# Last product of a decoder trunk: lower rows accumulated as two column halves, last four slices walked row half by row half

## The reference

```python
def rms_norm(x, g):
    return x * rsqrt(mean(x * x, axis=-1) + 1e-6) * g

def conformer_mixer(hn, ...):
    a, g, z = split(hn @ w_in + b_in)            # z has no bias
    u = depthwise_conv(a * sigmoid(g), w_dw) + b_dw      # 31 taps, causal
    u = silu(layer_norm(u, ln_g, ln_b))
    return (u * silu(z)) @ w_out + b_out         # w_out is 2048 x 2048
```

## Time and profile before

| | |
|---|---|
| three runs | 886.42, 886.36, 884.99 us; median 886.36 |
| profiled execution, first to last instruction | 883.1 us |
| what the median has around that | 3.3 us |
| TensorE busy | 860.6 us, 97% of the span |
| VectorE, ScalarE, GpSimd busy | 571.1, 437.5, 346.2 us |
| mean granted TensorE clock | 0.993 of full |
| slices 24 to 31 of the last product | 846.66 to 868.59 us |
| last byte of the last store | about 882.05 us |

### The profile page before, as it was taken

How to read it: one execution, slowest core, us unless ns; L and a number is a source line. 1 busy time by engine, 2 the same in 40 slices (tenths; PEclk the granted TensorE clock), 3 DMA queues, 4 the chain that set the end, 5 groups by cost and what they waited for, 6 DMA issues and landing times.

```text
span 883.1 us, 12265 instructions
## 1 busy us (share of the span) xinstructions
PE 860.6 (97%) x4061; PEld 713.4 (81%) x4061; DVE 571.1 (65%) x922; ACT 437.5 (50%) x603; POOL 346.2 (39%) x173
## 2 busy tenths in 40 slices
PE   9999999999999999999999899999999999899993
PEld 6788888888888888888888688888888888788882
DVE  5655455555555465555554749999999999556554
ACT  6745354454446444454444575444455554474441
POOL 0342004400440014400001588888888788670002
PEclk9999999999999999999999999999999999999997
DMA  9865656555665566646555255555555556447512
GB/s 308 295 191 149 186 161 195 172 168 161 190 176 158 158 182 185 187 142 237 191 191 191 95 187 193 183 179 178 183 185 190 190 162 202 162 164 265 190 48 95
DMA packets 97702, 159.49 MB, mean 181 GB/s; under 512 B 3237, under 2 KB 38917, under 8 KB 97285
## 3 DMA queue, kind: packets, MB, share of 16 engines
q1 hardware_dynamic: 97620, 159.04, 56.0%
q10 hardware_dynamic: 48, 0.02, 0.0%
HBM read 156.94 MB, written 2.10 MB: 180 GB/s over the span
## 4 chain that ended last, share of the span: by engine, by line
PE 94%; DVE 2%; DMA 2%; ACT 0%; POOL 0%; SPq 0%; issue 0%; DVEq 0%
PE acc L358 29%; PE acc L360 29%; PE acc L359 29%; PE X L370 3%; DMA raw<-in_w_in 1%; DVE xrow L996 1%; PE acc L414 1%; DMA xrow<-in_x 1%; PE X L460 1%; DVE c_row L1059 1%; PE X L470 0%; PE X L454 0%; PE X L453 0%; PE X L469 0%; PE X L468 0%; PE X L448 0%
## 5 line engine op out<-in xcount | busy, mean ns | idle before, releaser
L632 ACT ACTIVATE w_hi<-raw 128x1024 fp32r<-128x1024 f32 x288 | 305.2, 1060 | 379.8 <-PE acc L360 376.5
L870 DVE TENSOR_TENSOR w_lo<-raw,w_hi 128x1024 fp32r<-128x1024 f32 x184 | 245.0, 1333 | 235.9 <-ACT w_hi L632 235.6
L358 PE MATMUL acc<-w_hi,xT_hi 128*128 128x512 f32 x876 | 345.8, 395 | 0.8 <-DVE xT_lo L877 0.8
L360 PE MATMUL acc<-w_hi,xT_lo 128*128 128x512 f32 x876 | 341.5, 390 | 0.0
L359 PE MATMUL acc<-w_lo,xT_hi 128*128 128x512 f32 x876 | 341.0, 389 | 0.0
L1152 POOL TENSOR_TENSOR w_lo<-raw,w_hi 128x1024 fp32r<-128x1024 f32 x104 | 252.9, 2436 | 176.3 <-ACT w_hi L632 176.0
L360 PEld LDWEIGHTS acc<-w_hi,xT_lo 128*128 128x128 f32 x876 | 164.4, 188 | 34.9
L358 PEld LDWEIGHTS acc<-w_hi,xT_hi 128*128 128x128 f32 x876 | 164.6, 188 | 33.8 <-DVE xT_lo L877 1.2
L359 PEld LDWEIGHTS acc<-w_lo,xT_hi 128*128 128x128 f32 x876 | 164.7, 188 | 32.6
L1027 DVE SCALAR_TENSOR_TENSOR X<-u_pad,taps,X 128x256 f32<-128x256 f32 x464 | 182.6, 481 | 0.0
L1130 POOL TENSOR_TENSOR rope_t<-q_row,sin_t 128x256 f32<-128x256 f32 x16 | 15.3, 989 | 192.2 <-ACT q_row L640 192.2
(11 more groups left out here) (120 smaller groups left out, 645.1 us busy)
## 6 DMA issues: line engine op xcount, KB each, us to landing
raw<-in_w_in SPq DMA_DIRECT2D x78, 1024.0 KB, 5.3
raw<-in_w_in SPq DMA_DIRECT2D x68, 512.0 KB, 4.4
raw<-in_w_out SPq DMA_DIRECT2D x32, 1024.0 KB, 5.0
gpost<-in_post_g SPq DMA_DIRECT2D x2, 1024.0 KB, 4.6
xrow<-in_x SPq DMA_DIRECT2D x3, 512.0 KB, 9.7
out<-xrow SPq DMA_DIRECT2D x4, 320.0 KB, 3.6
bout<-in_b_out SPq DMA_DIRECT2D x1, 1024.0 KB, 6.8
xrow<-in_x SPq DMA_DIRECT2D x2, 256.0 KB, 4.0
```

What stands on the lines that cost most here:

```text
L358: nc.tensor.matmul(a, hi[:, k, rows], w_hi[:, slot, i], start=(k == 0), stop=False)
L360: last = nc.tensor.matmul(a, lo[:, k, rows], w_hi[:, slot, i], start=False, stop=(k == KT - 1))
L632: nc.scalar.activation(w_hi[:, slot], raw[:, u % LOADS, 2 * half:2 * half + 2], ACT.Copy).then_inc(hi_ready[slot], 1)
L870: nc.vector.tensor_tensor(w_lo[:, slot], raw[:, u % LOADS, 2 * half:2 * half + 2], rd(w_hi, slot), ALU.subtract).then_inc(lo_ready[slot], 1)
```

## The change

The change is in the last product alone, from slice 24 on (column block 3), and in what follows it.

- TensorE: the upper rows still go into `acc[:, 1, 0]` with 512-wide matmuls. The lower rows go into two other PSUM banks, `X[0]` for the left 256 columns of the block and `X[1]` for the right 256, with matmuls 256 wide (`HALVES`, `last_products`). In slices 24 to 27 each slice does upper rows, left half, right half. The last four slices, which fill the ring, are walked three times: upper rows of slices 28 to 31, then the left half of the lower rows of 28 to 31, then the right half. `row0_done` and `half_done` tell of each walk's end.
- The means, the roots and the residual of the two row halves are separate. The lower rows' squares of the last block come in two halves (`ssq_half`), and a small instruction (`part_half`) adds the left one to the mean ahead of the right one.
- VectorE does the whole residual, one row half at a time (`last_residual`): the upper rows in four parts of 512 columns, the lower rows in four of 768, 640, 384 and 256. ScalarE's scaling and GpSimd's addition are gone. SyncE stores each part by itself: eight stores of one row half.

```diff
-OUT_PARTS = [slice(0, 128), slice(128, 384), slice(384, 768), slice(768, 1088), slice(1088, 1408)]
-POOL_COLS = slice(OUT_PARTS[-1].stop, D)
+OUT_PARTS = ([slice(c, c + NCOL) for c in range(0, D, NCOL)],
+             [slice(0, 768), slice(768, 1408), slice(1408, 1792), slice(1792, D)])
+HALVES = (slice(0, NCOL // 2), slice(NCOL // 2, NCOL))
...
-            for n, c in enumerate(OUT_PARTS):
-                sp.wait_ge(o_ready, n + 1)
-                sp.dma_start(ov[:, :, c], xrow[:, :, c]).then_inc(stored, 16)
-                if n in (2, 3):
-                    sp.wait_ge(o_pool, n - 1)
-                    sp.dma_start(ov[:, n - 2, POOL_COLS], xrow[:, n - 2, POOL_COLS]).then_inc(stored, 16)
+            for m in range(MT):
+                for c in OUT_PARTS[m]:
+                    n += 1
+                    sp.wait_ge(o_ready, n)
+                    sp.dma_start(ov[:, m, c], xrow[:, m, c]).then_inc(stored, 16)
...
+            def last_products(s, m, bank, c):
+                slot = s % RING
+                pe.wait_ge(lo_ready[slot], rounds(S_OUT1, 0, 0, s))
+                for i in range(SL_K):
+                    k = SL_K * (s % SLICES) + i
+                    rows = slice(m * P, (m + 1) * P)
+                    nc.tensor.matmul(bank, vT_hi[:, k, rows], w_hi[:, slot, i, c], start=(k == 0), stop=False)
+                    nc.tensor.matmul(bank, vT_hi[:, k, rows], w_lo[:, slot, i, c], start=False, stop=False)
+                    last = nc.tensor.matmul(bank, vT_lo[:, k, rows], w_hi[:, slot, i, c], start=False,
+                                            stop=(k == KT - 1))
+                return last
...
-                slice_products(S_OUT1, 0, 0, s, vT_hi, vT_lo, by_row=(s == 4 * SLICES - 1))
+                if s < 3 * SLICES:
+                    slice_products(S_OUT1, 0, 0, s, vT_hi, vT_lo)
+                elif s < 4 * SLICES - RING:
+                    last_products(s, 0, acc[:, 1, 0], slice(0, NCOL))
+                    for j in range(2):
+                        last = last_products(s, 1, X[j][:, HALVES[j]], HALVES[j])
+                    last.then_inc(w_used[s % RING], 1)
...
+            for s in range(4 * SLICES - RING, 4 * SLICES):
+                last = last_products(s, 0, acc[:, 1, 0], slice(0, NCOL))
+            last.then_inc(row0_done, 1)
+            for j in range(2):
+                for s in range(4 * SLICES - RING, 4 * SLICES):
+                    last = last_products(s, 1, X[j][:, HALVES[j]], HALVES[j])
+                last.then_inc(half_done, 1)
...
-            for m in range(MT):
-                part = yg1[:, m, POOL_COLS]
-                nc.scalar.activation(part, part, ACT.Copy, scale=rms[3][:, m:m + 1]).then_inc(scaled, 1)
+            squares(junk1[:], y1[:, 0, last_col:D], 0, NG - 1, 30)
+            for j in range(2):
+                act.wait_ge(y_ready, MT * (NG - 1) + 2 + j)
+                act.wait_ge(ssq_ready, 31 + j)
+                c = slice(last_col + HALVES[j].start, last_col + HALVES[j].stop)
+                nc.scalar.activation(junk1[:, 0:NCOL // 2], y1[:, 1, c], ACT.Square, accum_out=ssq_half[:, j:j + 1]
+                                     ).then_inc(ssq_ready, 1)
...
-            out1_biased(NG - 1, 1)
-            mean_with_last(32, 2)
-            out1_gained(NG - 1, 1)
+            last_mean(31, 0)
+            last_biased(0)
+            last_gained(0)
             dve.wait_ge(rms_ready, 4)
-            dve.wait_ge(yg_ready, MT * NG)
-            for c in OUT_PARTS:
-                residual(c, 3, yg1, o_ready)
+            dve.wait_ge(yg_ready, MT * (NG - 1) + 1)
+            for c in OUT_PARTS[0][0:3]:
+                last_residual(0, c)
+            dve.wait_ge(ssq_ready, 32)
+            nc.vector.scalar_tensor_tensor(out=part_half, in0=ssq_half[:, 0:1], scalar=1.0 / D,
+                                           in1=mean_part[:, 1:2], op0=ALU.mult, op1=ALU.add).then_inc(half_part, 1)
+            last_biased(1)
+            last_residual(0, OUT_PARTS[0][3])
+            last_gained(1)
+            dve.wait_ge(ssq_ready, 33)
+            dve.wait_ge(half_part, 1)
+            nc.vector.scalar_tensor_tensor(out=mean_sq[:, 1:2], in0=ssq_half[:, 1:2], scalar=1.0 / D,
+                                           in1=part_half, op0=ALU.mult, op1=ALU.add).then_inc(ms_ready, 1)
+            dve.wait_ge(rms_ready, 5)
+            dve.wait_ge(yg_ready, MT * NG + 1)
+            for c in OUT_PARTS[1]:
+                last_residual(1, c)
...
-            inverse_root(rms[3], mean_sq, ms_ready, 4, rms_ready)
             for m in range(MT):
-                pool.wait_ge(scaled, m + 1)
-                c = xrow[:, m, POOL_COLS]
-                nc.gpsimd.tensor_tensor(c, c, yg1[:, m, POOL_COLS], ALU.add).then_inc(o_pool, 1)
+                inverse_root(rms[3][:, m:m + 1], mean_sq[:, m:m + 1], m_half[:, m:m + 1], ms_ready, 4 + m, rms_ready)
```

More of the change, by code:

```diff
@@ L151, in build @@
         mean_part = small[:, 110:112]
+        ssq_half = small[:, 112:114]
+        part_half = small[:, 114:115]
         rms = [small[:, 12 + 2 * i:14 + 2 * i] for i in range(4)]
@@ L230, in build @@
         part_ready = sem("part_ready")
-        scaled = sem("scaled")
-        o_pool = sem("o_pool")
+        half_done = sem("half_done")
+        half_part = sem("half_part")
         stored = sem("stored")
@@ L1072, in out1_biased @@
             def out1_biased(n, m):
-                if n == NG - 1 and m == 0:
+                if n == NG - 1:
                     dve.wait_ge(row0_done, 2)
@@ L1098, in _, with last_residual @@
             out1_gained(NG - 1, 0)
-            out1_biased(NG - 1, 1)
-            mean_with_last(32, 2)
-            out1_gained(NG - 1, 1)
-            dve.wait_ge(rms_ready, 4)
-            dve.wait_ge(yg_ready, MT * NG)
-            for c in OUT_PARTS:
-                residual(c, 3, yg1, o_ready)
+            def last_residual(m, c):
+                nc.vector.scalar_tensor_tensor(
+                    out=xrow[:, m, c], in0=yg1[:, m, c], scalar=rms[3][:, m:m + 1], in1=xrow[:, m, c],
+                    op0=ALU.mult, op1=ALU.add).then_inc(o_ready, 1)
@@ new lines, in last_mean, with last_biased @@
+            def last_mean(ready, m):
+                dve.wait_ge(ssq_ready, ready)
+                dve.wait_ge(part_ready, 2)
+                nc.vector.scalar_tensor_tensor(out=mean_sq[:, m:m + 1], in0=ssq[:, m, NG - 1:NG], scalar=1.0 / D,
+                                               in1=mean_part[:, m:m + 1], op0=ALU.mult, op1=ALU.add
+                                               ).then_inc(ms_ready, 1)
+            last_mean(31, 0)
+            def last_biased(j):
+                dve.wait_ge(half_done, j + 1)
+                c = slice((NG - 1) * NCOL + HALVES[j].start, (NG - 1) * NCOL + HALVES[j].stop)
+                nc.vector.tensor_tensor(y1[:, 1, c], X[j][:, HALVES[j]], bout[:, c], ALU.add).then_inc(y_ready, 1)
@@ new lines, in last_gained @@
+            def last_gained(j):
+                dve.wait_ge(y_ready, MT * (NG - 1) + 2 + j)
+                c = slice((NG - 1) * NCOL + HALVES[j].start, (NG - 1) * NCOL + HALVES[j].stop)
+                nc.vector.tensor_tensor(yg1[:, 1, c], y1[:, 1, c], gpost1[:, c], ALU.mult).then_inc(yg_ready, 1)
+            last_biased(0)
+            last_gained(0)
+            dve.wait_ge(rms_ready, 4)
+            dve.wait_ge(yg_ready, MT * (NG - 1) + 1)
+            for c in OUT_PARTS[0][0:3]:
+                last_residual(0, c)
@@ L1112, in _, with inverse_root @@
             pool.wait_ge(const_set, 2)
-            def inverse_root(out_, in_, ready, count, done):
+            def inverse_root(out_, in_, power, ready, count, done):
                 pool.wait_ge(ready, count)
-                nc.gpsimd.tensor_tensor(out_, in_, m_half, ALU.pow).then_inc(done, 1)
-            inverse_root(rms[0], mean_sq, ms_ready, 1, rms_ready)
+                nc.gpsimd.tensor_tensor(out_, in_, power, ALU.pow).then_inc(done, 1)
+            inverse_root(rms[0], mean_sq, m_half, ms_ready, 1, rms_ready)
             pool.wait_ge(rope_in, 48)
@@ L1156, in _ @@
                 low(S_AG, 0, 16, s)
[L1157 removed]
+            inverse_root(rms[1], mean_sq, m_half, ms_ready, 2, rms_ready)
             for s in range(RING - 1, 10):
                 low(S_AG, 0, 16, s)
[L1160 removed]
+            inverse_root(rms[2], mean_sq, m_half, ms_ready, 3, rms_ready)
             for s in range(10, 2 * SLICES):
```

12 lines of the change are left out of this document (5 added, 7 removed).

## The result

| | before | changed |
|---|---|---|
| runs, us | 884.99 to 886.42 (4) | 879.11, 879.40, 879.68, 879.82 |
| median, us | 885.88 | 879.54 |
| profiled execution, first to last instruction | 883.1 | 877.5 |
| from the last matmul's end to the end | 14.5 | 8.0 |

The ratio of the changed kernel to the one before is 0.9928, 95% interval 0.9916 to 0.9941: faster by 6.3 us, where 880.8 (5.6 less) was forecast. In the three comparisons behind this one the kernel before ran 37 more times, with medians of 885.4, and the changed kernel five more, with 879.77 and 0.9934 [0.992, 0.9947]. Against 885.4 the gain is 5.6 to 5.9 us, so part of the 6.3 is the scatter of four runs.

What follows compares the result with a forecast made beforehand. TensorE's stream and the tail behind it bound the kernel: stream +0.6, to residual 2.86 to 2.4, residual and issue 5.96 to 1.96, stores 4.64 to 2.88; span 877.5 plus 3.27 gives 880.8 us, range 879.3 to 883.3.

Steps and rivals of the forecast that it cites:

- TensorE's stream: Slices 24 to 31: 256-wide matmuls start every 0.120 us, adding 0.64 us; the stream's last product ends at 869.22.
- the load of the earlier trace: Kernel before, at 106.61: a weight load whose matmul began about 0.12 later, taken as the narrow matmul's pitch.
- Rivals 1, 2 and 4: Narrow matmuls, us: 1: load unhidden 890.3, 5%; 2: plain-f32 rate 912, 1%; 4: load partly hidden 884.6 to 888.1, 5%.
- Slice 31's cover: Upper rows' walk: slice 31 wanted at 861.94, its split ready at 860.44, a cover of 1.5 us.
- The third rival: Tail: upper rows' work too late, store phase still 1.7 MB or slice 31 a us late; 882.6 us, 10%.
- Last matmul to residual: Tail, from TensorE's end to the start of the residual: 2.86 us becomes 2.4.
- the root: GpSimd, lower rows' tail: 0.70 us with no VectorE work beside it; the other end is 1.07.
- Residual, issue, stores: Tail: residual up to the store phase with issue, 5.96 becomes 1.96 us; store phase 4.64 becomes 2.88 at 364 GB/s.
- The sum within the trace: Whole profiled span: 869.3 + 8.2 = 877.5 us against 883.09, -5.6.
- From span to time: Whole kernel: median of runs lies 3.27 us above the profiled span, left as it is, giving 880.8.
- the forecast's own range: Whole kernel's time: 879.8 to 882.3 us, from matmul pitch, root at 1.07 and run scatter; forecast 79%.
- the range for 8 in 10: Whole kernel's time: 879.3 to 883.3 us, taking in the third rival and a matmul pitch up to 0.14.

Runs made afterwards that it cites:

- the repeat: The changed kernel run once more with no edit, beside its variants: 879.77 us, ratio 0.9934 to the kernel before.

## Why the prediction was right

**TensorE's stream.** The number was right, 0.120 per narrow matmul, and the stream 22.64 us against 22.56. That the same figure came from the load of the earlier trace rows was luck: with the halves of 384 and 128 columns the distance is columns at 2.4 GHz plus 0.013, the 0.0133 by which the 0.2267 of 512 columns exceeds 512/2.4 GHz, and 0.1067 + 0.0133 = 0.120 needs no load. The whole of the load's record was not waited for. The rule that the Trainium skill gives in "TensorE: Matmul & The Clock Gate", Part 3, by which a load overlaps only when it goes to another row group, doesn't hold here: at 256 and 384 columns the load is hidden, at 128 there is a floor of 0.112, not a sum of load and matmul. Part 3 also names a second case in which a load is pulled ahead, one into the background weight buffer; no run here shows whether that is what happens. Rivals 1, 2 and 4 fall with the 0.120.

**Slice 31's cover.** The timeline of VectorE shows the split that the earlier trace rows had at 858.89:

```profile
859.48 1.23 DVE L903 TENSOR_TENSOR w_lo<-raw,w_hi 128x1024 fp32r<-128x1024 f32 x1 [1.59 <-ACT w_hi L662]
```

It is done at 860.71 and was wanted at about 862.2. The third rival's late slice didn't come, nor its late upper rows. But the margin was thinner than I wrote. The fourth upper store is issued at 870.65, 2.1 us before the first of the lower rows and not over 3, and the transfers of the upper rows end at about 872.4, 1.2 us before the lower rows' begin and not 2.

**Last matmul to residual.** Predicted 2.39, measured 871.70 - 869.51 = 2.19. The right half's bias add started 0.03 behind the last matmul, and VectorE's queue was ready at that same moment, as worked out. The term that was off is the root: 0.70 was taken from the 128 x 2 roots of the earlier trace rows; one column takes 0.55 when VectorE leaves it alone. That it would not be the 1.07 was argued from what stood beside it, and the gain multiply put ahead of the mean shows that.

**Residual, issue, stores.** From the residual's start to the store phase 1.98 against 1.96, and the store phase 2.72 at 371 GB/s against 2.88 at 364. End 1.10 against 1.04.

**The sum within the trace.** +0.7 stream, -0.7 to the residual, -4.0 to the store phase, -1.9 in it, +0.1 at the end, and +0.2 that slice 24 started later: -5.6, a span of 877.5 as predicted. The agreement to a tenth is luck, since small misses cancel and the repeat spans 878.8; that the sum from slice 24 on is 30.6 against the predicted 877.5 - 846.66 = 30.8 is not. By the variants, taken in this order, of the 5.8 us from slice 24 on (36.4 - 30.6), 2.6 come from the residual being VectorE's alone, 1.4 from the row halves apart, 2.3 from the long walk that lets the upper rows be stored early, and -0.5 from the column halves. The prediction had TensorE's price of the halves but never set the tail's gain against it by itself.

**From span to time.** This is the step that failed by size. I put 886.36 - 883.1 = 3.27 around the span. In every later pair of an execution's span and its own time, 1.75 to 1.9 lie around it (879.4 and 877.5 of the changed kernel, 884.97 and 883.1 of a later run of the one before): the profiled execution was among the faster ones, not the median one (the 37 later ones span 882.7 to 885.6, with a median of 883.6). So 1.4 us of scatter were taken for a constant, and 880.8 came out 1.3 above the measured 879.54, which lies below the forecast's own range (879.8 to 882.3) and 0.2 inside the range for 8 in 10.

## What to carry to other kernels

Ask of a tail split over three engines whether the helpers slow the main one: here VectorE alone did 4096 columns sooner than it had done 2816 beside GpSimd. Keep the order of work that lets half of the output be stored under the last product, and leave small GpSimd steps on the path without a VectorE operation on SBUF beside them. Narrowing the last matmuls is worth it only if what it takes off the tail exceeds 0.013 us for each matmul added, or more where a floor like the 0.112 at 128 columns is reached.

## What the runs showed of the hardware that I had not expected

- VectorE slows GpSimd only by some operations: a 128 x 1 power took 0.55 us alone and beside an addition out of PSUM, 1.00 beside a residual piece with all operands in SBUF. The 128 x 2 one took 0.69 alone and 1.07 beside a multiply of SBUF operands. The addition out of PSUM is one case in one trace.
- It goes the other way and harder: the 384-wide residual piece takes 0.61 us alone and 1.88 beside GpSimd's 640-wide addition, and ends 0.42 behind the addition's end both times.
- A matmul on rounded-fp32 operands costs 0.013 us over its columns at 256, 384 and 512 columns; at 128 it takes 0.112, which is 0.045 more than that sum.
- A small first store doesn't bring the stream forward by its lead: 131 KB are gone in 0.4 us, and the engines are empty until the next part's issue has taken its 0.9 us.
